# Moving the low halves of the split weights, and the rows, against the 128-byte grid of the on-chip memory

## The reference

```python
def swiglu(h, w_in, w_out):
    gate, up = jnp.split(h @ w_in, 2, axis=-1)
    return (jax.nn.silu(gate) * up) @ w_out
```

## Time and profile before

| | |
|---|---|
| profiled execution | 2409.69 us, of which the span is 2407.9 us |
| median of three runs | 2411.97 us |
| TensorE matmuls | busy 2370.9 us, 98% of the span |
| VectorE | busy 1557.6 us, 65% |
| ScalarE | busy 1209.4 us, 50% |
| DMA | 398.39 MB, mean 165 GB/s |
| granted TensorE clock | 1.000 over the span |

### The profile page before, as it was taken

One profiled execution on the slowest core, in us unless ns is written; L12 is line 12 of the kernel. 1 busy time (PEld: TensorE's weight loads), 2 busy tenths in 40 slices (PEclk: granted clock), 3 DMA queues, 4 the chain that ended last, 5 costly groups with the idle time before them and its releaser, 6 DMA issues.

```text
span 2407.9 us, 39768 instructions
## 1 busy us (share of the span) xinstructions
PE 2370.9 (98%) x14322; PEld 2029.7 (84%) x14322; DVE 1557.6 (65%) x2316; ACT 1209.4 (50%) x1783; POOL 158.1 (7%) x145
## 2 busy tenths in 40 slices
PE   8999999999999999999999999999999999999999
PEld 6756888888898868888888899998888889989887
DVE  5386665423474267766876858777677776777875
ACT  4365422222353234655554586565455556865553
POOL 3000100000000000000000013100000000221000
PEclk9999999999999999999999999999999999999999
DMA  9453755433363214656656655366566565545654
GB/s 332 135 184 128 228 154 162 143 107 96 99 193 96 88 53 154 204 163 195 201 173 193 192 168 176 130 181 193 178 191 193 180 196 167 183 130 158 200 174 149
DMA packets 388420, 398.39 MB, mean 165 GB/s; under 512 B 17344, under 2 KB 382432, under 8 KB 388304
## 3 DMA queue, kind: packets, MB, share of 16 engines
q1 hardware_dynamic: 381984, 377.67, 50.8%
q0 software_dynamic: 6320, 19.17, 2.6%
HBM read 395.73 MB, written 1.05 MB: 165 GB/s over the span
## 4 chain that ended last, share of the span: by engine, by line
PE 84%; DVE 5%; ACT 4%; issue 3%; POOL 2%; SPq 1%; DMA 1%; DVEq 0%; ACTq 0%; POOLq 0%
PE acc L1086 30%; PE acc L1097 23%; PE acc L1090 16%; PE acc L1163 2%; PE wk L1163 2%; ACT w_hi L1689 1%; DVE w_lo L2328 1%; SPq L795 1%; PE wk L1285 1%; PE acc L1639 1%; PE wk L1323 1%; PE acc L1323 1%; PE wk L1305 1%; POOL bias L994 1%; PE wk L1534 1%
## 5 line engine op out<-in xcount | busy, mean ns | idle before, releaser
L2328 DVE TENSOR_TENSOR w_lo<-raw,w_hi 128x1024 fp32r<-128x1024 f32 (+1 forms) x656 | 815.9, 1258 | 496.9 <-ACT w_hi L1689 495.1
L1689 ACT CAST w_hi<-raw 128x1024 fp32r<-128x1024 f32 (+1 forms) x650 | 663.8, 1034 | 466.8 <-PE acc L1097 346.1
L1086 PE MATMUL acc<-h_room,w_hi 128*128 128x512 f32 x2328 | 584.6, 393 | 2.0 <-DVE h_room L2579 0.8
L1097 PE MATMUL acc<-h_room,w_lo 128*128 128x256 f32 (+1 forms) x3688 | 562.0, 294 | 0.0
L1097 PEld LDWEIGHTS acc<-h_room,w_lo 128*128 128x128 f32 x3688 | 515.5, 188 | 44.7
L1086 PEld LDWEIGHTS acc<-h_room,w_hi 128*128 128x128 f32 x2328 | 415.5, 188 | 79.0 <-DVE h_room L2456 3.3
L1090 PE MATMUL acc<-h_room,w_hi 128*128 128x256 f32 (+1 forms) x2720 | 464.6, 323 | 3.2 <-POOL h_room L999 2.2
L1090 PEld LDWEIGHTS acc<-h_room,w_hi 128*128 128x128 f32 x2720 | 399.9, 188 | 47.7 <-issue 6.6
L1086 PE MATMUL acc<-hid_all,w_hi 128*128 128x512 f32 x880 | 221.4, 392 | 0.0
L1086 PEld LDWEIGHTS acc<-hid_all,w_hi 128*128 128x128 f32 x880 | 156.7, 188 | 26.7
L1097 PEld LDWEIGHTS acc<-hid_all,w_lo 128*128 128x128 f32 x1056 | 152.3, 188 | 16.7
(11 more groups left out here) (439 smaller groups left out, 2300.6 us busy)
## 6 DMA issues: line engine op xcount, KB each, us to landing
raw<-in_w_in_dram SPq DMA_DIRECT2D x100, 512.0 KB, 4.0
raw<-in_ffn_w_in_dram SPq DMA_DIRECT2D x88, 512.0 KB, 4.4
raw<-in_ffn_w_gate_dram SPq DMA_DIRECT2D x88, 512.0 KB, 4.2
raw<-in_ffn_w_up_dram SPq DMA_DIRECT2D x88, 512.0 KB, 4.3
raw<-in_ffn_w_down_dram SPq DMA_DIRECT2D x80, 512.0 KB, 4.0
raw<-in_ret_w_qkvg_dram SPq DMA_DIRECT2D x48, 512.0 KB, 3.6
raw<-in_ffn_w_out_dram SPq DMA_DIRECT2D x40, 512.0 KB, 3.5
ring<-in_ada_w_dram SPq DMA_DIRECT2D x34, 512.0 KB, 4.7
```

The costliest lines, as they stand in the source:

```text
L1086: pe.matmul(outs[cb], w_hi[:, s, k, c], merged[:, :, kk, t], start=(u == 0 and k == 0), stop=False, skip_group_check=True)
L1097: mm = pe.matmul(o, w_lo[:, s, k, cb * P:(cb + 1) * P], x[:, u * KCH + k, t], start=False, stop=(last and k == nk - 1), skip_group_check=True)
L1689: act.copy(w_hi[:, s, 0:nk, :], raw[:, s, 0:nk, :]).then_inc(hi_done, 1)
L2328: dve.tensor_tensor(w_lo[:, s, 0:nk, :], raw[:, s, 0:nk, :], w_hi[:, s, 0:nk, :], ALU.subtract).then_inc(lo_done, 1)
```

## The change

It allocates 64 bytes (`line`) between `w_hi` and `w_lo`. All that is allocated behind moves along by 64 bytes: `w_lo`, `xT`, `h_room` and everything after it, the tiles that share an area with `hid_all` included. The first layer's rows are then read at shift `LINE` instead of 0. `ring` is cut in two parts, so that its last four slots, which lie over `w_lo`, move along with it.

```diff
         with ExitStack() as on:
-            ring = sb("ring", [P, 3 * SLOTS, KCH, COLS], F32, on)
+            ring01 = sb("ring01", [P, 2 * SLOTS, KCH, COLS], F32, on)
+            sb("ring_line", [P, LINE], F32, on)
+            ring2 = sb("ring2", [P, SLOTS, KCH, COLS], F32, on)
         raw = sb("raw", [P, SLOTS, KCH, COLS])
         w_hi = sb("w_hi", [P, SLOTS, KCH, COLS], F32R)
+        sb("line", [P, LINE])
         w_lo = sb("w_lo", [P, SLOTS, KCH, COLS], F32R)
...
+        def ring_slot(n):
+
+            return ring01[:, n] if n < 2 * SLOTS else ring2[:, n - 2 * SLOTS]
...
-        h_all = rows_at(0)
+        h_all = rows_at(LINE)
         h_hi, h_lo = h_all[:, 0], h_all[:, 1]
...
-            return ring[:, SLOTS + n % 2 * SLOTS + n // 2] if n < 2 * SLOTS else ada_in[:, n - 2 * SLOTS]
+            return ring_slot(SLOTS + n % 2 * SLOTS + n // 2) if n < 2 * SLOTS else ada_in[:, n - 2 * SLOTS]
...
-            return {"extra": extra, "ring": ring, "late": late}[tile][:, n]
+            return ring_slot(n) if tile == "ring" else {"extra": extra, "late": late}[tile][:, n]
```

## The result

The kernel after takes 2432.62 us, the median of four runs (2431.84 to 2433.58), against 2411.79 us for the kernel before: a ratio of 1.0089, 95% interval 1.0077 to 1.0101. It is slower by 21 us, where 7.8 us of gain were forecast. The profiled execution took 2431.89 us, its span is 2430.1 us.

The account below looks back on a forecast made before the run. The prediction took TensorE's matmuls to bound the kernel, their pitch depending on operand addresses. Its terms, −9.3 + 0 + 3.1 + 1.2 − 2.8 = −7.8 us, gave 2401.9 us for the profiled execution and 2404.2 for the median; range 2399 to 2429.

Parts of the forecast that it names:

- 0/0: Stationary and moving operand both on a multiple of 128 bytes: 226.7 ns at 512 columns, 120.0 at 256.
- Item 1: Merged units, rows from 64 to 0, `w_lo` from 0 to 64: 2733.3 ns instead of 2756.5, × 401 = −9.3 us.
- Item 2: Single units of 256 tokens: 2826.7 ns against 2827, nothing, as `w_lo` gains what `w_hi` loses.
- Item 3: 58 single units of 512 tokens in the first layer: +53.3 ns each, +3.1 us; 8 units of `rk`: nothing.
- Item 4: `dn0`, whose rows go from 0 to 64: 24 × 2.3 ns × 22 = +1.2 us.
- Item 5: Wide products, stationary rows from 64 to 0: −2.1 us with moving high halves, −0.7 with low ones, together −2.8 us.
- Item 6: Everything else, such as VectorE's subtraction, full float32 matmuls and landing slots: costed at nothing, given between −1 and +2 us.
- rows on a multiple bring back the 120 ns: Matmuls of 256 columns, moving rows on a multiple, cost 120.0 ns whatever the weights do: +13.7 us, 2426; chance 0.20.
- Two pieces on a multiple cost the 233.3: Moving operands in two pieces put merged `w_hi` matmuls at 233.3 ns: about +14 us, 2426; chance 0.08.
- The low halves keep what they have: `w_lo` matmuls of 256 columns take 115.7 ns in merged units, −6.2 us there; 2409 us in all; chance 0.15.
- 64/0: Stationary operand 64 bytes off a multiple of 128, moving one on it: 233.3 ns at 512 columns, 113.3 assumed at 256.
- rival of no effect: Independent ports keep weight loads and moving reads apart, so the shift changes nothing: 2412 us; chance 0.07.

Follow-up runs that it names:

- the rows really in step: The kernel after with 128 bytes more ahead of the rows, so they lie at 0 from `w_hi` and 192 from `w_lo`: 2427.63 us, ratio 1.0068.
- the first experiment: A small kernel of its own, TensorE on zeros, not the reference's work, varying the distance between moving and stationary operands: pitches and whole units timed, no kernel time.

## Why the prediction was wrong

The bound was right: TensorE's pitch is the whole of it, and its dependence on addresses was seen in the trace of before. Two steps failed.

The first is how the prediction named a case, "by the offsets from a multiple of 128 bytes". The rows that it took for 0/0 lie 128 bytes from `w_hi`.

The second is the price of the merged unit, which is wrong for the case that was meant, too: 226.7 ns for the high halves, taken from 48 like matmuls in a row, and 113.3 for the low ones, taken from a pattern ("which leaves 0 at 256"). The experiment with the rows really in step has the distances that the prediction had in mind. Its merged unit takes 2780 ns and not 2733, as 8 × 230 and 8 × 117.5 (of the 47 ns between them some 18 are of the high halves and 29 of the low ones), and its time is 2427.6 us and not 2404.2. So of the 28.4 us by which the forecast missed 2432.6, the wrong prices make 23.4 and the wrong period 5.0. Both conditions under which the forecast called itself wrong came true: the low halves had 117.5 ns in two units of three, and the merged high ones went up from 229 to 232.5.

Measured terms below come from the mean unit of each form in the two traces.

- *Item 1, merged units, −9.3 us forecast.* Measured 2.760 to 2.792 us for the 291 units on normal rows and 2.762 to 2.790 for the 110 on hidden rows: +12.4 us. Its line 7 × 226.7 + 233.3 + 7 × 113.3 + 120.0 = 2733 gives the high halves 1820 ns and the low ones 913. Measured are 1858 and 933: 38 ns more for the rows at 128 from `w_hi`, for which the first experiment has 232.6, and 20 more for the low halves, from which the rows lie 64 as before, so that two units of three keep the slower pitch. This item alone is off by 21.7 us, of 30.5 in all the items.
- *Item 2, single units of 256, 0 forecast.* Measured +28 ns in the mean unit, × 104 = +3.0 us: 2840 ns settled for 2827, and none of the 12 units that had the better rhythm of 2720.
- *Item 3, first layer, +3.1 and `rk` 0.* Measured +113 ns × 58 = +6.6 and +73 × 8 = +0.6. The 16 high ones went to 232.5 as well, which "rows stay at 0" had left alone: they stayed against the grid, and moved against `w_hi`. A settled unit of the first layer takes 5565 ns for 5440; some 94 of the 125 are of the high halves and 31 of the low ones, for which 53 had been forecast. That the total of low halves was not far off is luck: 233.3 was the price of distance 192, and they lie at 64.
- *Item 4, `dn0`, +1.2.* Measured about +50 ns × 22 = +1.1. Here the hidden rows really are 64 from `w_hi` and the price was right.
- *Item 5, wide products, −2.8.* Measured 233.3 to 231.1 in the 384 matmuls of `rv`, and 1.1 ns less in the other 96: −1.0. With the rows as the stationary operand, distance 192 became 128 for the moving high halves and stayed 192 for the low ones. In two pieces the first experiment has 233.5 and 233.2 for these, so no gain; what gives the mixed order its 231.1 isn't shown.
- *Item 6, the rest, 0.* Right: the split takes 1280 ns for 1279 and no new wait shows.

The sum of the measured terms is +22.7 us, against 22.2 in the spans.

Of the rivals, *rows on a multiple bring back the 120 ns* had the sign and was 6.6 us low, with the wrong cause: its loss was to be in the 256-column matmuls, and most of it came in those of 512. *Two pieces on a multiple cost the 233.3* gave nearly the measured 232.5 for merged high halves, but two pieces are within 1 ns of one, and the first layer with one piece slowed as well. *The low halves keep what they have* named the mechanism, "the distance of the two operands would be all that counts", and I set it aside because of "the 233.3 of 64/0, which isn't 229". That row was the clue and not the objection. With the rows stationary the distance is −64, which modulo 256 is 192, and the small kernel has 233.4 there. The three places that the trace had, 0/0, 0/64 and 64/0, were three distances: 0, 64 and 192. The fourth, 128, stood in no row, and I took it for 0 because I had reduced by 128. (That rival also holds a slip: at its own 115.7 ns the single units cost +19 ns and not +33, and it comes to 2407 us.)

The Trainium skill's page "SBUF — State Buffer" (section "A bandwidth-pool intuition that's wrong (but worth ruling out)") states a second, independent read port for the weight loads. The rival of no effect, which the prediction drew from it, isn't borne out: with one operand fixed, the other one's address alone moves the pitch from 226.7 to 234.4 ns. Whether the ports have a part in that no run shows.

## What to carry to other kernels

Reduce an observed dependence on addresses to differences before pricing a shift, and don't assume a period that no row shows: two offsets that agree modulo 128 may differ modulo 256. A small kernel of TensorE alone, on zeros, in the real unit's form, gives the price of an arrangement mostly within some 5 ns of 2800, if it runs for enough units to settle; a pitch from a long stretch doesn't, since in a unit of 8 and 8 the matmuls don't come down to it. The wrong prices cost more here than the wrong period did. And a price that no row shows is better measured first than continued from a pattern of two pairs. After any change of allocation, list the distance of each pair of operands, those of tiles that merely come later too.

## What the hardware showed that was not expected

- The pitch of fp32r matmuls with a load each depends on the distance between moving and stationary address modulo 256 bytes: 226.7 to 234.4 ns at 512 columns, 116.8 to 120.0 at 256 in steady stretches with the weights on a multiple. It is signed (64: 228.9, 192: 233.4 at 512 columns), and the two lengths don't want the same distance (0 is the best at 512 and, with 96 and 128, the worst at 256). 226.7 ns are 544 cycles at the granted 2.4 GHz.
- At some distances there are two steady rhythms for the same addresses, 113.3 and 117.8 ns at 256 columns, and one matmul of another length ahead picks which (units of 2720 or 2827 ns, and it holds for the whole stretch). With single units at (64, 192) only the better one was seen.
- What makes it so is not shown. The runs tell that no other engine is needed for it (in the small kernel VectorE is busy 1% and the DMA engines idle) and that moving both operands by 64 bytes left the pitch as it was, with two exceptions: distance 192 at 256 columns, and the 12 single units that lost the better rhythm. In both the two values are those of the two rhythms.
